# Hybrid decoder layer on one core: low-rank up-projections and running sums issued inside the first key, receptance and value slabs, and the first slabs laid out by the contraction and loaded in halves

## What is computed

```python
proj = x @ w_in[l]                              # (256, 2048) @ (2048, 6432)
mixed = p + (_token_shift(p) - p) * mu          # p: the RWKV columns of proj
r, k, v, w_d, a_d, g_d = jnp.split(mixed, splits, axis=-1)   # widths 1024 x3, 64, 64, 160
w = -jax.nn.softplus(-(w0 + jnp.tanh(w_d) @ w_up)) - 0.5
decay = jnp.exp(-jnp.exp(w))
a = jax.nn.sigmoid(a0 + a_d @ a_up)
g = jax.nn.sigmoid(g_d) @ g_up
kk = heads(k * k_k)
kk = kk / jnp.maximum(jnp.sqrt(jnp.sum(jnp.square(kk), -1, keepdims=True)), 1e-12)
k = k * (1.0 + (a - 1.0) * k_a)
# state update per token with decay, kk, a, k, v; read out with r; group norm; gate g
# rotary q, k; A = softmax(q1 k1) - lambda * softmax(q2 k2); A @ v; RMS norm per head
x = LN(alpha * x + concat(y_rwkv, y_diff) @ w_out[l])
x = LN(alpha * x + square(relu(x @ w_ff1[l])) @ w_ff2[l])
```

## Time and profile before

| | |
|---|---|
| median of 3 runs | 1323.35 us |
| the profiled execution, its own time | 1328.44 us |
| its span, first to last instruction | 1326.7 us |
| mean granted clock of the matrix engine | 0.986 |
| DVE, ACT, GpSimd busy | 738.2, 567.2, 82.3 us |
| HBM traffic | 218.83 MB read, 2.10 MB written |

### The profile page before, as it was taken

How to read it: one execution, slowest core, us unless ns; L and a number is a source line. 1 busy time by engine, 2 the same in 40 slices (tenths; PEclk the granted TensorE clock), 3 DMA queues, 4 the chain that set the end, 5 groups by cost and what they waited for, 6 DMA issues and landing times.

```text
span 1326.7 us, 24389 instructions
## 1 busy us (share of the span) xinstructions
PE 1273.9 (96%) x10200; PEld 1096.8 (83%) x10200; DVE 738.2 (56%) x762; ACT 567.2 (43%) x615; POOL 82.3 (6%) x53
## 2 busy tenths in 40 slices
PE   6999999999999889989999999999999999999995
PEld 6899999999777767877888888888888888888884
DVE  4367766363575135677555555555555555655557
ACT  4643444445554123454333333333344444444443
POOL 0021112000000010029200000000000000000000
PEclk9999999999999899999999999999999999999998
DMA  8254565223300234564555555555565555555541
GB/s 325 101 195 163 187 221 192 96 101 101 126 32 5 109 148 145 197 229 146 193 179 183 188 188 190 189 184 179 183 252 192 192 191 194 196 197 188 194 160 64
DMA packets 33671, 222.02 MB, mean 167 GB/s; under 512 B 4773, under 2 KB 5157, under 8 KB 7742
## 3 DMA queue, kind: packets, MB, share of 16 engines
q1 hardware_dynamic: 33598, 220.94, 47.2%
HBM read 218.83 MB, written 2.10 MB: 167 GB/s over the span
## 4 chain that ended last, share of the span: by engine, by line
PE 90%; DVE 5%; ACT 3%; issue 2%; DMA 0%; SPq 0%; DVEq 0%; ACTq 0%
PE ps L447 89%; DVE wlo L1362 1%; DVE x1f L1736 0%; DMA stage<-w_in 0%; ACT whi L1054 0%; DVE stats L1701 0%; DVE xres L1806 0%; PE ps L707 0%; DVE xres L1700 0%; DVE xres L1804 0%; ACT L1054 0%; DVE acts L1750 0%; ACT xres L1054 0%; ACT kr L1054 0%; DVE yt L1659 0%
## 5 line engine op out<-in xcount | busy, mean ns | idle before, releaser
L1362 DVE TENSOR_TENSOR wlo<-stage,whi 128x2048 fp32r<-128x2048 f32 x192 | 447.9, 2333 | 429.4 <-ACT whi L1054 428.3
L447 PE MATMUL ps<-acts,whi 128*128 128x256 f32 (+1 forms) x2400 | 622.8, 337 | 16.7 <-DVE wlo L1362 14.8
L1054 ACT ACTIVATE whi<-stage 128x2048 fp32r<-128x2048 f32 x194 | 371.8, 1917 | 593.5 <-PE ps L447 590.5
L447 PE MATMUL ps<-acts,wlo 128*128 128x256 f32 x1712 | 483.8, 283 | 0.5 <-issue 0.5
L447 PEld LDWEIGHTS ps<-acts,whi 128*128 128x128 f32 x2400 | 409.5, 191 | 72.9 <-issue 20.8
L447 PEld LDWEIGHTS ps<-acts,wlo 128*128 128x128 f32 x1712 | 327.2, 191 | 0.7 <-issue 0.7
L447 PE MATMUL ps<-whi,shi 128*128 128x512 f32 x632 | 249.5, 395 | 2.8 <-DVE slo L1673 2.7
L447 PE MATMUL ps<-wlo,shi 128*128 128x512 f32 x632 | 248.0, 392 | 0.0
L447 PE MATMUL ps<-whi,slo 128*128 128x512 f32 x632 | 247.8, 392 | 0.0
L447 PEld LDWEIGHTS ps<-whi,shi 128*128 128x128 f32 x632 | 119.5, 189 | 35.7 <-issue 6.8
L447 PEld LDWEIGHTS ps<-wlo,shi 128*128 128x128 f32 x632 | 119.5, 189 | 25.4
(11 more groups left out here) (206 smaller groups left out, 839.4 us busy)
## 6 DMA issues: line engine op xcount, KB each, us to landing
stage<-w_ff SPq DMA_DIRECT2D x128, 1024.0 KB, 4.9
stage<-w_in SPq DMA_DIRECT2D x51, 1024.0 KB, 4.9
stage<-w_out SPq DMA_DIRECT2D x16, 1024.0 KB, 4.9
xstage<-xT SPq DMA_DIRECT2D x4, 512.0 KB, 7.0
xres<-x SPq DMA_DIRECT2D x1, 2048.0 KB, 7.8
gain<-ln_gain SPq DMA_DIRECT2D x2, 1024.0 KB, 8.0
bias<-ln_bias SPq DMA_DIRECT2D x2, 1024.0 KB, 10.1
out<-xres SPq DMA_DIRECT2D x8, 256.0 KB, 2.2
```

What stands on the lines that cost most here:

```text
L447: return pe.matmul(out, lhsT, rhs, start=start, stop=stop, skip_group_check=True)
L1054: return act.activation(out, in_, func, **kw)
L1362: TTn(wlo[k0 % NHL][:, :], stage[k0 % NST][:, :], f(whi[k0 % NHL][:, :]), ALU.subtract).then_inc(s_lo, 1)
```

## The change

1. The low-rank columns are laid out by the contraction: each slab holds 16 blocks of 128 columns, three blocks for each of the 16 contraction steps in turn. All three products gather in banks 4, 5 and 6 (before in 0, 1 and 2), and all three are complete only with slab 2. The three slabs are loaded, and split by ACT and DVE, in two halves of 1024 columns.
2. DVE writes a tile of zeros, and the matrix engine begins with `WARM` = 18 float32 matmuls of 256 columns on it, into bank 7.
3. The low-rank stage is taken apart: its matmuls are issued by `low_rank` at half-slab positions inside slabs 4 to 7. ACT's and DVE's parts are moved to match: the split of slab 3 stands ahead of the scaling of the low-rank products, the sigmoids and exponentials between the splits of chunks 0 to 2, `gam` is copied per j, the rotary angles go to chunk 6, the sines to chunk 7.
4. Sums, root, first reciprocal and `bonus_and_kk` of a j come later by one chunk: both `BD` matmuls after c=2, root and first reciprocal in c=0 of the next j, `bonus_and_kk(j-1)` in front of c=1. For the last j they stand behind the loop and in slab q=1 of the query and key slabs; `FIRST_SLAB` is (2, 9), before (1, 8). `sig` and a few waits (`eyes`) move along.

```diff
+WARM = 18
-        FIRST_SLAB = (1, 8)
+        FIRST_SLAB = (2, 9)
@@ SyncE: half slabs
+            def half_slabs(n):
+                sp.dma_start(stage[n][:, 0:SLAB // 2], t["w_in"][n][:, 0:SLAB // 2]).then_inc(s_half[n], 16)
+                sp.dma_start(stage[n][:, SLAB // 2:SLAB], t["w_in"][n][:, SLAB // 2:SLAB]).then_inc(s_stage[n], 16)
             x_piece(0)
-            slab(0, 0, t["w_in"][0])
-            for j in range(1, 4):
-                x_piece(j)
-            slab(1, 1, t["w_in"][1])
+            half_slabs(0)
+            x_piece(1)
+            half_slabs(1)
+            x_piece(2)
+            x_piece(3)
+            half_slabs(2)
...
@@ matrix engine
+            def low_rank(g, part):
+                at_half = 2 * (g - G_MIX) + part
+                if at_half == 2:
...
+                    pe.wait_ge(s_free, 2)
+                    for a in range(TT_):
+                        for q in range(2):
+                            mm(ps[:, 4 + 2 * a + q, :], wt[:, tok(a)], wup[:, 512 * q:512 * q + 512]).then_inc(s_z, 1)
+                items = {3: range(0, 4), 4: range(4, 8), 5: (8, 9), 6: (10, 11), 7: (12, 13), 8: (14, 15)}
+                for n in items.get(at_half, ()):
...
+            def chunk(b0, g, k0):
+                for s in range(2):
+                    w = (k0 + s) % NHL
+                    halves_ready(g + s)
+                    for j in range(8):
+                        if j % 4 == 0:
+                            low_rank(g + s, j // 4)
...
-            chunk(0, 0, 0, ready=(s_xlo, 1))
-            chunk(2, 2, 2, width=128, slabs=1)
...
+            pe.wait_ge(s_zero, 1)
+            for _ in range(WARM):
+                mm(ps[:, 7, 0:2 * P], zeros[:, 0:P], zeros[:, P:3 * P])
+            for n in range(16 * N_LORA):
+                g, j = divmod(n, 16)
+                k, fb = divmod(n, 3)
+                if j == 0:
+                    pe.wait_ge(s_hih, g + 1)
+                    pe.wait_ge(s_loh, g + 1)
+                if j == 8:
+                    halves_ready(g)
+                if k % 4 == 0 and fb == 0:
+                    pe.wait_ge(s_xlo, k // 4 + 1)
...
-                    if c == 1:
+                    if c == 2:
+                        if j == 0:
+                            pe.wait_ge(s_itemd, 2 * NB)
+                        pe.wait_ge(s_rk, j + 1)
                         pe.wait_ge(s_sq, j + 1)
                         mm(ps[:, 4 + j % 2, :], BD, sqt[:, :, :]).then_inc(s_ss, 1)
-                    if c == 2:
-                        pe.wait_ge(s_rk, j + 1)
                         mm(ps[:, 6 + j % 2, :], BD, rkt_[:, :, :]).then_inc(s_bon, 1)
@@ ScalarE, chunk loop
+                    if m == 1:
+                        items(4, 10)
+                    if m == 2:
+                        items(12, 16)
                     hi(g + 2, g + 2)
+                    if m == 0:
+                        decay_sigmoids()
+                        items(0, 4)
+                    if c == 0 and j:
+                        kk_roots(j - 1)
+                    if m == 7:
+                        sines()
...
+                    if m == 1:
+                        items(10, 12)
                     hi(g + 3, g + 3)
@@ VectorE, chunk loop
-                    if c == 0 and j:
+                    if m == 6:
+                        angles()
+                    if c == 1 and j:
                         bonus_and_kk(j - 1)
                     if c == 1:
+                        if j == 0:
+                            dve.wait_ge(s_itemd, NB)
...
                     lo(g + 2, g + 2)
-                    if c == 2:
...
+                    if c == 0 and j:
+                        kk_inverses(j - 1)
+                    if m == 8:
+                        sines_signed()
                     lo(g + 3, g + 3)
...
-            bonus_and_kk(NB // 2 - 1)
+            kk_inverses(NB // 2 - 1)
...
+                if q == 1:
+                    bonus_and_kk(NB // 2 - 1)
```

More of the change, by code:

```diff
@@ L465, in pairs @@
                     last.then_inc(s_used, 1)
-            def chunk(b0, g, k0, width=256, slabs=2, ready=None):
-                kts = SLAB // width
-                for s in range(slabs):
+            def low_rank(g, part):
+                at_half = 2 * (g - G_MIX) + part
+                if at_half == 2:
+                    pe.wait_ge(s_cst, 16)
+                    pe.wait_ge(s_lup, 32)
+                    pe.wait_ge(s_lora, 1)
+                    pe.wait_ge(s_vec, 1)
+                    pe.wait_ge(s_free, 2)
[4 more added lines that the diff above has]
+                for n in items.get(at_half, ()):
+                    b, bk = n % NB, 4 + n % 4
+                    if n < 4:
+                        pe.wait_ge(s_sig, n + 1)
+                    else:
+                        pe.wait_ge(s_itemd, n - 3)
+                    if n < NB:
+                        mm(ps[:, bk, 0:S], aup[64:128, P * b:P * b + P], wa[64:128, :]).then_inc(s_item, 1)
+                    else:
+                        for a in range(TT_):
+                            last = mm(ps[:, bk, 256 * a:256 * a + 256], sig[:, a, P * b:P * b + P],
+                                      cst[:, C_SU:C_SU + 2 * P])
+                        last.then_inc(s_item, 1)
@@ L472, in chunk @@
+            def chunk(b0, g, k0):
+                for s in range(2):
                     w = (k0 + s) % NHL
                     halves_ready(g + s)
[L474 to L478, removed]
+                    for j in range(8):
+                        if j % 4 == 0:
+                            low_rank(g + s, j // 4)
+                        k = s * 8 + j
+                        for fb in range(2):
@@ L503, in rows @@
                 last.then_inc(s_used, 1)
[L506 to L529 removed]
+            pe.wait_ge(s_zero, 1)
[11 more added lines that the diff above has]
+                    pe.wait_ge(s_xlo, k // 4 + 1)
+                w, cols, acc = g % NHL, slice(P * j, P * j + P), ps[:, 4 + fb, 0:S]
+                mm(acc, whi[w][:, cols], acthi[:, k, :], start=(k == 0), stop=False)
+                mm(acc, whi[w][:, cols], actlo[:, k, :], start=False, stop=False)
+                last = mm(acc, wlo[w][:, cols], acthi[:, k, :], start=False, stop=(k == KT - 1))
+                if j == 15:
+                    last.then_inc(s_used, 1)
             for j in range(NB // 2):
@@ L1372, in x_lo, with lo_half @@
                     ALU.subtract).then_inc(s_xlo, 1)
+            def lo_half(n, part):
+                dve.wait_ge((s_hih, s_hi)[part], n + 1)
+                if n == 2:
+                    dve.wait_ge(s_used, 1)
+                cols = slice(SLAB // 2 * part, SLAB // 2 * part + SLAB // 2)
+                TTn(wlo[n % NHL][:, cols], stage[n][:, cols], f(whi[n % NHL][:, cols]), ALU.subtract
+                    ).then_inc((s_loh, s_lo)[part], 1)
+            dve.memset(zeros[:, :], 0.0).then_inc(s_zero, 1)
             dve.memset(wt[64:65, :], 1.0)
             x_lo(0)
-            lo(0, 0)
-            for j in range(1, 4):
-                x_lo(j)
-            lo(1, 1)
+            lo_half(0, 0)
+            lo_half(0, 1)
+            x_lo(1)
+            lo_half(1, 0)
+            lo_half(1, 1)
+            x_lo(2)
+            x_lo(3)
+            lo_half(2, 0)
+            lo_half(2, 1)
             dve.wait_ge(s_vecl, 16)
```

147 lines of the change are left out of this document (83 added, 64 removed).

## The result

The changed kernel takes 1347.0 us (median of 4 runs, 1345.68 to 1351.43) where the kernel before takes 1323.52 (4 runs, 1322.83 to 1326.43): 1.0184 times as long, 95% interval 1.015 to 1.0218. It is slower, as forecast, but by 23.5 us and not by 11.7, and it lies above the range of 1325.5 to 1341.5. The profiled execution took 1351.43 us, the slowest of its four; its span is 1349.6. Executions of one kernel differ by 3.6 and 5.8 us in these two groups and by 12 to 15 us in larger ones further on.

What follows compares the result with a forecast made beforehand. The matrix engine was taken as the bound. Terms -1.0 (start and slab 4) + 9.3 (receptance chunks) + 3.0 (clock) + 0.4 (solves) = +11.7 on 1323.35 gave 1335.0 us; the range leaving out 2 in 10 was 1325.5 to 1341.5.

Steps and rivals of the forecast that it cites:

- What bounds the kernel: Whole kernel: the matrix engine is the bound, busy 1273.9 of 1326.7 us, every other engine under 60%.
- The start: First slabs: real work begins at 12.2 us behind the zeros (bounds 9.4 and 17); slab 2 ends at 29.5, not 31.34.
- Slab 4: Before slab 4: a wait of 2.9 us instead of 1.72; term with the earlier start -1.0 us (-3.8 to +3.9).
- the table chain: Theory listed with the experiments, for the front: slab 4's split comes late because of sigmoids and table load.
- The receptance chunks: Chunks m = 4, 7, 10: vector work and GpSimd delay a split; three waits of 3.1 us, +9.3 us (2.7 to 16).
- The clock: Behind four waits of about 3 us: two are followed by the low level (1.2 GHz), +3.0 us (0 to +6).
- cold clock: Theory listed with the experiments, for the front: the low clock level behind waits carries most of it.
- The solves: Solves: the second turn's 0.4 us wait goes, one of about 0.8 comes in the first; +0.4 us (0 to +1).
- At nothing: Rotary angles, small loads held by the exponentials, root and first reciprocal: covered, cost 0; uncovered, each under 1 us.
- Rival A: Receptance chunks: small instructions do not wait for GpSimd, only the split is slower; +5.3, 1328.7 us; chance 0.26.
- B: Start: matmuls on zeros are cheap, under 0.2 us each; sum +1.4, 1325 us, not slower; chance 0.12.
- C: Start: zeros leave the clock low, so triples after them may start low too; total 1340 to 1342 us; chance 0.05.

Runs made afterwards that it cites:

- GpSimd held back: The changed kernel with one more wait on GpSimd, so its products begin only after the receptance chunk's first split: 1329.47 us, ratio 1.0040.
- the moved condition alone: The kernel before with one edit, `bonus_and_kk(j-1)` in front of the receptance chunk (c=1) instead of the key chunk (c=0): 1342.14 us, ratio 1.0112.
- both repaired: The changed kernel with the bonus behind the first split, decay matmuls ahead of slab 4's wait, slab 3 loaded before the small tables: 1326.05 us, ratio 1.0033.
- zeros alone: The kernel before with one edit, 18 matmuls on zeros in front of the first slab: 1324.57 us, ratio 1.0007.
- zeros and earlier split: The kernel before with the 18 matmuls on zeros and slab 4's split ahead of the sines on ScalarE and signed sines on VectorE: 1320.78 us, ratio 1.0002.
- both repaired without zeros: The changed kernel with bonus behind the first split, decay matmuls ahead of slab 4's wait, slab 3 loaded first, and `WARM = 0`: 1323.38 us, ratio 1.0004.
- the earlier split alone: The kernel before with only slab 4's split moved ahead of the sines on both engines, no zeros: 1322.44 us, ratio 0.9992.

## Why the prediction was off

**What bounds the kernel, and that this change costs: right.** Every loss is a wait of the matrix engine or its clock.

**The start: right.** Forecast 12.2, triples 0.36 apart from there, slab 2 over at 29.5; measured 10.95, 0.36, 28.6. The zeros were 9.98 us for 18, 0.55 each, where I had them at 10.9 in all. The low level lasted for nine of the 36 records of the zeros, to 5.3 us (their starts are 0.43 us apart till then and 0.215 from there on), so for about 4 us and not for 6.

**Slab 4: the wait right in sum, the clock not.** 2.9 us were forecast, 0.87 + 1.71 came. The 0.87 stands before slab 3, whose load landed only at 25.06 behind the small tables; I had not looked for it. The chain to slab 4's split ran as forecast, 8.56 us from the last low-rank triple (28.57) to 37.13, for 8.65. Its start and its high split on the scalar engine:

```profile
28.67 0.47 ACT L1087 ACTIVATE wa<-ps,vec 128x256 f32<-128x256 f32 x1 [1.70 <-PE ps L458]
...
32.81 1.90 ACT L1087 ACTIVATE whi<-stage 128x2048 fp32r<-128x2048 f32 x1
```

The low split behind it ends at 37.03. This is the table chain, and the trace bears it out. Without the fall of the clock (as in the run with GpSimd held back) the mark at 89.73 is 0.6 us early, for a forecast of -1.0; with it, 1.66 late.

**The receptance chunks: mechanism right, size wrong.** This is the first of the two terms that failed: 3 x 3.1 = 9.3 forecast, 3 x 4.8 = 14.4 measured, near the 5.3 that the text kept for "all four products slip in". The step at fault is that `ki` would wait once, for the first product, and `bt` once. In fact each of the four small instructions waited for one product: the first `ki` for the first, the second `ki` of the pair for the second, `bt` for the third, the last `ki` for the fourth. I had let the second `ki` pass right behind the first, and let `bt` and `ki` run in one piece. With 0.9 as the base (0.8 measured) and four turns of about 1.0 us, the sum is 4.9.

On this the Trainium skill, "SBUF — State Buffer", section "Who interferes with whom", speaks of an exclusive lock that is held for the whole instruction. The trace agrees now for the small instructions too: 0.72 became 2.51, 0.43 became 1.55, 0.68 became 1.75, and the product with an operand in PSUM stayed at 0.68. In this case the two engines take turns instruction by instruction. Instructions of 0.43 and 0.68 us lost 1.12 and 1.07, so their number counted here and not their length.

**The clock: too small.** This is the second term that failed, and by more: 3.0 forecast (0 to 6), 9.6 measured. The step at fault is the choice that two of four waits would be followed by the low level, at 1.5 us each, the price of the one low stretch of the earlier trace rows. In the profiled execution all four were, three of them for 6.8 us: 3.2 us at slab 4 (6.8 us at half speed are 3.4; the marks against the run with GpSimd held back give 3.1) and 6.4 in the rounds. With waits of 3.94 us (the moved condition alone) the three rounds lost 5.7, 5.7 and 6.9, so 1.8 to 2.9 beyond the wait; with 4.8 us they lost 7.07, 7.51 and 6.27, so 1.5 to 2.7 beyond it; with 1.8 us they lost 3.6, 2.1 and 3.6, so 0.3 to 1.8 beyond it; with 0.8 us and no low level 1.1 each, 0.2 beyond it. In each round the loss beyond the wait is, within 0.3 us, half of the time that the matrix engine worked at the low level; the round with 2.1 had none. So the theory called cold clock falls short: in the rounds the clock carries 6.4 of 20.85 us, the waits 14.4.

**The solves: +0.4 forecast;** the wait there is 1.0 in place of 0.4. **At nothing: right.** No other wait appears up to 330 us but the 0.87 by "issue" at 255.29, in a solve.

The sum with the measured sizes, for the profiled execution: -2.0 (start and slab 4 by the starts, 37.13 + 14.0 against 53.15) + 3.2 + 14.4 + 6.4 + 0.6 = 22.6, against 22.99. The two terms that failed, 5.1 us too small in the waits and 6.6 in the clock, make 11.7 of the 11.8 by which the forecast was short. Rival A fell on the length of `ki`, B on the 0.55 us of a zero matmul, C on the 0.36 at 11.50.

## What to carry to other kernels

Before moving small vector instructions, ask what GpSimd starts in that moment. Where a signal set GpSimd going here and small vector instructions with their operands in SBUF followed it, each of them waited for one whole GpSimd instruction, and the one that must be ready (here a split) belonged ahead of them. Either order the signal behind the urgent instruction or make the other engine wait for it; one line did it here. And price a wait of the matrix engine with the lower clock that may come with it, of which only what is worked through costs: here 4.8 us cost 6.3 to 7.5.

## What the runs showed beside

**A lead in the front of the program did not show in the time.** The four versions with both repairs or with zeros (both repaired, zeros alone, zeros and earlier split, both repaired without zeros) are 2 to 6 us ahead of before at 90 to 390 us in their traces, and so is the earlier split alone (3.0). The intervals of the four leave no room for such a gain; that of the earlier split alone does. Two things were found beside it, and neither settles it.

The first is the clock. The mean granted clock of the kernel before is 0.9881 (27 runs) and 0.9893 (23, on another chip); beside them the zeros alone have 0.9857, zeros and earlier split 0.9861, both repaired 0.9862, the earlier split alone 0.9866 and both repaired without zeros 0.9870. A mean lower by 0.0019 to 0.0027 over 1320 us is 2.5 to 3.6 us of full speed, about what the front gives. The traces give no one place for it. Here are before, then zeros with the earlier split, then zeros alone, the same stretch:

```profile
420.00:620.00 200.00, 178.92 (x1924) 146.28 (x1922) 106.15 (x124) 72.56 (x86) 34.73 (x25) 0.95 0.42 154
```

```profile
420.00:620.00 200.00, 182.73 (x1902) 151.64 (x1892) 107.40 (x123) 73.63 (x85) 40.72 (x28) 0.92 0.44 159
```

```profile
420.00:620.00 200.00, 177.57 (x1923) 146.69 (x1922) 107.16 (x124) 72.26 (x86) 36.63 (x25) 0.95 0.43 154
```

One has more of the low level there and one has not. And in the traces the lead is not lost: the earlier split alone is 2.9 us ahead at 386.8 and 2.8 at the end (spans of 1323.9 and 1326.7). But the profiled execution of before, 1328.44 us, is slower than every other run of it on record, and each profile is one execution. So whether the clock takes the lead back stayed open.

The second is that the matrix engine, busy without a gap and at full clock, has two paces in the large MLP stage. First before, then the kernel with zeros alone:

```profile
700.00:740.00 40.00, 40.00 (x229) 34.69 (x228) 20.82 (x15) 15.36 (x11) 0.00 (x0) 1.00 0.53 184
```

```profile
700.00:740.00 40.00, 40.00 (x233) 35.24 (x232) 22.39 (x16) 14.87 (x11) 0.00 (x0) 1.00 0.55 192
```

229 matmuls against 233 is 1.7%. The starts of the low splits say the same: nine slabs take 50.9 us (708.49 to 759.37) in before and 49.9 (705.11 to 755.03) with zeros alone, and over the stage it comes to about 6 us. The profiles of both repaired, of zeros alone and of zeros with the earlier split have the faster pace; those of the change and of all the others have the slower one. Runs of the kernel before alone lie between 1316 and 1328 us, in keeping with two paces that an execution falls into. A lead of 2 to 4 us is smaller than that step. What decides between the paces stayed open as well.
